# One layer of a hybrid decoder on one core: the column spans of its dense products

## The reference, cut to what matters

```python
xn = rmsnorm(x, attn_norm_g)
gq, gk, gv, gg, glr, dq, dk, dv = split(xn @ w_in)          # 1024 x 3088
log_a = log_sigmoid(glr @ w_gk2 + b_gk) / 16                # rank 16
gla_o = gated_linear_attention(gq, gk, gv, log_a)           # 4 heads
diff_o = differential_attention(rope(rmsnorm(dq)), rope(rmsnorm(dk)), dv)   # 4 heads, paged cache for the samples
h = x + concat(rmsnorm(gla_o) * silu(gg), rmsnorm(diff_o) * 0.8) @ w_out    # 1024 x 1024
hn = rmsnorm(h, ffn_norm_g)
h = h + (silu(hn @ w_ffn_gate) * (hn @ w_ffn_up)) @ w_ffn_down              # 1024 x 2816, twice, and back
gate = sigmoid(rmsnorm(h, ple_norm_g) @ w_ple_gate)         # 1024 x 1024
h = h + gate * (p @ w_ple_proj)                             # 256 x 1024
```

## Time and profile before

| | |
|---|---|
| median of 3 runs | 2168.06 us (2166.67 to 2168.38) |
| span of the profiled execution | 2161.1 us |
| median less span | 7.0 us |
| TensorE matmuls | busy 1927.8 us, 13348 instructions |
| VectorE, ScalarE, GpSimd | busy 972.4, 605.6, 404.4 us |
| mean granted TensorE clock | 0.943 |

### The profile page before, as it was taken

One profiled execution on the slowest core, in us unless ns is written; L12 is line 12 of the kernel. 1 busy time (PEld: TensorE's weight loads), 2 busy tenths in 40 slices (PEclk: granted clock), 3 DMA queues, 4 the chain that ended last, 5 costly groups with the idle time before them and its releaser, 6 DMA issues. The chain is left out here.

```text
span 2161.1 us, 36230 instructions
## 1 busy us (share of the span) xinstructions
PE 1927.8 (89%) x13348; PEld 1743.4 (81%) x13348; DVE 972.4 (45%) x1364; ACT 605.6 (28%) x1011; POOL 404.4 (19%) x398
## 2 busy tenths in 40 slices
PE   5999998556887789888789899999999999999798
PEld 4999998543555566656589899999999999999798
DVE  4224611784666545555533523433343334335543
ACT  4113312531444444444432211111111111112420
POOL 1112321331000234343311100110111011102210
PEclk9999999785878999999999999999999999999899
DMA  4323521005300799999721111111111111110221
GB/s 130 102 80 101 154 70 50 21 3 192 113 1 0 247 378 387 387 387 387 250 61 40 49 49 39 49 40 50 39 48 42 49 40 39 50 50 20 66 75 42
DMA packets 187844, 236.56 MB, mean 109 GB/s; under 512 B 12994, under 2 KB 127635, under 8 KB 187731
## 3 DMA queue, kind: packets, MB, share of 16 engines
q1 hardware_dynamic: 167250, 167.81, 24.3%
q0 software_dynamic: 20480, 67.13, 8.4%
HBM read 213.49 MB, written 16.92 MB: 107 GB/s over the span
## 5 line engine op out<-in xcount | busy, mean ns | idle before, releaser
L150 PE MATMUL psum<-h_hi,w_hi 128*128 128x364 f32 x1248 | 279.2, 332 | 2.5 <-issue 2.5
L150 PE MATMUL psum<-h_lo,w_hi 128*128 128x364 f32 x1248 | 276.6, 330 | 0.0
L150 PE MATMUL psum<-h_hi,w_lo 128*128 128x364 f32 x1248 | 275.4, 329 | 0.0
L2051 ACT ACTIVATE w_hi<-w_raw 128x1024 fp32r<-128x1024 f32 x66 | 68.9, 1060 | 584.4 <-PE psum L150 566.1
L150 PEld LDWEIGHTS psum<-h_hi,w_hi 128*128 128x128 f32 x1248 | 215.6, 189 | 4.6 <-issue 4.4
L150 PEld LDWEIGHTS psum<-h_lo,w_hi 128*128 128x128 f32 x1248 | 217.5, 189 | 0.0
L150 PEld LDWEIGHTS psum<-h_hi,w_lo 128*128 128x128 f32 x1248 | 217.1, 189 | 0.0
L2027 POOL TENSOR_TENSOR w_raw<-w_raw,gains 128x1024 f32<-128x1024 f32 x42 | 80.3, 1913 | 652.2 <-DMA w_raw<-in_w_ffn_gate 352.2
L150 PE MATMUL psum<-x_hi,w_hi 128*128 128x364 f32 x792 | 187.6, 345 | 11.1 <-DVE x_lo L1884 7.3
L1081 POOL DMA_DIRECT2D dec_v<-in_cache_v x256 | 138.0, 539 | 266.4 <-issue 263.3
L150 PE MATMUL psum<-x_hi,w_lo 128*128 128x364 f32 x792 | 176.4, 331 | 0.0
(11 more groups left out here) (268 smaller groups left out, 2831.3 us busy)
## 6 DMA issues: line engine op xcount, KB each, us to landing
dec_v<-in_cache_v POOLq DMA_DIRECT2D x256, 256.0 KB, 5.7
dec_k<-in_cache_k SPq DMA_DIRECT2D x256, 256.0 KB, 8.8
w_raw<-in_w_in SPq DMA_DIRECT2D x25, 512.0 KB, 3.9
w_raw<-in_w_ffn_gate SPq DMA_DIRECT2D x22, 512.0 KB, 3.9
w_raw<-in_w_ffn_up SPq DMA_DIRECT2D x22, 512.0 KB, 3.8
w_raw<-in_w_ffn_down SPq DMA_DIRECT2D x22, 512.0 KB, 4.1
feat_swap<-feat_n SPq DMA_DIRECT2D x32, 136.5 KB, 2.4
x_in<-in_x_prompt SPq DMA_DIRECT2D x4, 1024.0 KB, 8.1
```

The source lines that it names most:

```text
L150: ins = pe.matmul(out[:, c, 0:SPAN], w(k), x(k)[:, c * SPAN:c * SPAN + SPAN], start=n == 0 and w is whi and x is xhi, stop=n == len(ks) - ...
L2051: act.activation(m.whi[:, slot], m.raw[:, u], ACT.Copy).then_inc(s["w_hi"], 1)
```

## The change

The 1092 columns of a dense product are cut at 512 and 1024: the spans have 512, 512 and 68 columns. The first two fill their banks wholly, so the three banks hold 1092 adjacent elements, and every evacuation reads them as one run. Number, operands and order of the matmuls are the same. L454 and the row sums (L1711) keep pieces of 364.

```diff
-def spans(ap):
-
-    return ap.rearrange("p (c n) -> p c n", n=SPAN)
+CUTS = [(0, 512), (512, 512), (1024, T - 1024)]
+
+
+def whole(bank):
+
+    return bank.rearrange("p c n -> p (c n)")[:, 0:T]
...
-            for c in range(3):
-                ins = pe.matmul(out[:, c, 0:SPAN], w(k), x(k)[:, c * SPAN:c * SPAN + SPAN],
+            for c, (at, width) in enumerate(CUTS):
+                ins = pe.matmul(out[:, c, 0:width], w(k), x(k)[:, at:at + width],
                                 start=n == 0 and w is whi and x is xhi, stop=n == len(ks) - 1 and w is wlo)
...
-                    act.activation(spans(m.f[:, u]), dense[u][:, :, 0:SPAN], ACT.Copy).then_inc(evacuated, 1)
+                    act.activation(m.f[:, u], whole(dense[u]), ACT.Copy).then_inc(evacuated, 1)
...
-                for c in range(3):
-                    ins = pe.matmul(dense[pr][:, c, 0:SPAN], m.gk2[:, pr * P:pr * P + P],
-                                    m.g[0:16, low, c * SPAN:c * SPAN + SPAN], start=True, stop=True)
+                for c, (at, width) in enumerate(CUTS):
+                    ins = pe.matmul(dense[pr][:, c, 0:width], m.gk2[:, pr * P:pr * P + P],
+                                    m.g[0:16, low, at:at + width], start=True, stop=True)
...
-                dve.tensor_tensor(spans(m.h[:, n]), spans(m.h[:, n]), dense[n % 2][:, :, 0:SPAN], ALU.add
+                dve.tensor_tensor(m.h[:, n], m.h[:, n], whole(dense[n % 2]), ALU.add
                                   ).then_inc(s["evacuated"], 1)
```

More of the change, by code:

```diff
@@ L391, in _ @@
                 else:
-                    act.activation(spans(m.g[:, 0, :]), dense[0][:, :, 0:SPAN], ACT.Copy).then_inc(evacuated, 1)
+                    act.activation(m.g[:, 0, :], whole(dense[0]), ACT.Copy).then_inc(evacuated, 1)
                 hi(s + 2, u)
@@ L397, in _ @@
                     act.wait_ge(product_done, s + 1)
-                    act.activation(m.g[:, bass.ds(2 * i + (1 + v), 1), :].rearrange("p o (c n) -> p (o c) n", n=SPAN),
-                                   dense[1 - v][:, :, 0:SPAN], ACT.Copy).then_inc(evacuated, 1)
+                    act.activation(m.g[:, bass.ds(2 * i + (1 + v), 1), :].rearrange("p o t -> p (o t)"),
+                                   whole(dense[1 - v]), ACT.Copy).then_inc(evacuated, 1)
                     hi(s + 2, 1 - v)
@@ L403, in _ @@
                 act.wait_ge(product_done, s + 1)
-                act.activation(spans(m.g[:, s - 16, :]), dense[s % 2][:, :, 0:SPAN], ACT.Copy).then_inc(evacuated, 1)
+                act.activation(m.g[:, s - 16, :], whole(dense[s % 2]), ACT.Copy).then_inc(evacuated, 1)
         @block.tensor
@@ L696, in _ @@
                 act.wait_ge(s["z_done"], pr + 1)
-                act.activation(spans(m.t1[:, pr]), dense[pr][:, :, 0:SPAN], ACT.Abs, bias=gain(m, "bgk")[:, pr:pr + 1]
+                act.activation(m.t1[:, pr], whole(dense[pr]), ACT.Abs, bias=gain(m, "bgk")[:, pr:pr + 1]
                                ).then_inc(s["sp_abs"], 1)
@@ L880, in _ @@
                 dve.wait_ge(s["sp_abs"], pr + 1)
-                dve.tensor_scalar(spans(m.t2[:, pr]), dense[pr][:, :, 0:SPAN], gain(m, "bgk")[:, pr:pr + 1], 0.0,
+                dve.tensor_scalar(m.t2[:, pr], whole(dense[pr]), gain(m, "bgk")[:, pr:pr + 1], 0.0,
                                   ALU.add, ALU.min).then_inc(s["sp_min"], 1)
@@ L2145, in scaled @@
                 dve.wait_ge(s["product_done"], x + 1)
-                dve.tensor_tensor(spans(dst), dense[bank][:, :, 0:SPAN], spans(m.rb[:, :]), ALU.mult
+                dve.tensor_tensor(dst, whole(dense[bank]), m.rb[:, :], ALU.mult
                                   ).then_inc(s["evacuated"], 1)
@@ L2401, in scaled @@
                 dve.wait_ge(s["gate_done"], n + 1)
-                dve.tensor_tensor(spans(m.gt), dense[0][:, :, 0:SPAN], spans(m.rb[:, :]), ALU.mult
+                dve.tensor_tensor(m.gt, whole(dense[0]), m.rb[:, :], ALU.mult
                                   ).then_inc(s["gate_scaled"], 1)
@@ L2409, in result @@
                     dve.wait_ge(s["filled"], n * 3 + (PT - 3))
-                dve.tensor_tensor(spans(m.gp[:, u]), spans(m.gt), dense[1][:, :, 0:SPAN], ALU.mult
+                dve.tensor_tensor(m.gp[:, u], m.gt, whole(dense[1]), ALU.mult
                                   ).then_inc(s["gated"], 1)
```

## The result

The changed kernel takes 2356.7 us (median of 4 runs, 2353.57 to 2362.37), the kernel before 2168.16 (4 runs, 2166.67 to 2168.38): a ratio of 1.0881, with a 95% interval of 1.0864 to 1.0898. It is slower by 188.5 us; 186 were forecast, and 2354 us.

The account below looks back on a forecast made before the run. TensorE's dense matmuls (L150) were taken as the bound: 2616 groups of three at +73 ns give +191 us, less 5 us hidden in waits, so 2168 + 186 = 2354 us; range 2295 to 2419 us.

Parts of the forecast that it names:

- TensorE's pace in L150 is the whole of it: Dense products: 2616 groups of three matmuls take 1305 us of the span, and TensorE waits for nothing in it.
- The load needs 107 to 112 ns and lies under the short matmul alone: Dense products: the next weight load fits only under the 68 columns, so that matmul takes 112 ns, not 28.3.
- The wide slots: Each 512-column matmul of the dense products was taken as 230 ns, between a floor of 213 and 234.
- the two readings: The extra beyond streaming columns: fixed at 14.6 ns gives 228 ns for 512 columns, growing with columns gives 234.
- The sum: Three matmuls sharing weights: 572 ns against 499, +191 us over 2616 groups, less 5 us filling TensorE's waits at stage starts.
- The 7.0 us around the program: Median 2168.06 us lies 7.0 us over the span of 2161.1; this was taken as around the program and staying.
- The evacuations are free: PSUM evacuations: one run of 1092 elements in place of three of 364 gives nothing, taken as 0.
- What would show it: FFN profile signs: groups 0.57 us apart, about 0.11 after the 68-column start, 7848 loads, tile of 72 matmuls 13.7 us.
- The hidden load: Rival, dense products: TensorE holds more than one load ahead, so no change, 2168 us; chance 0.08.
- The half load: Rival, dense products: a float32r load needs one cycle a column, short slot 58 ns, about 2215 us; chance 0.06.
- plain float32: Rival, dense products: narrow float32r runs in two passes with a load each, short slot 224 ns, 2647 us; chance 0.03.
- The clock: Rival, dense stages: granted clock falls to half for a tenth of the time, some +125 us on top; chance 0.01.

Follow-up runs that it names:

- The four widths: Last matmul of 68, 132, 196 or 240 columns in place of the kernel before's 364, evacuation in one run: 2356.7, 2283.8, 2215.0 and 2165.8 us.
- 288: Spans of 288, 512 and 292 columns, evacuated in one run, against the kernel before with three of 364: 2166.4 us, ratio 0.9999.
- 292: Spans of 292, 512 and 288 columns, evacuated in one run, against the kernel before with three of 364: 2165.2 us, ratio 0.9998.

## Why the prediction was right

*TensorE's pace in L150 is the whole of it.* Right: 207 us more of TensorE's busy time (by records that overlap), 194 us more of span, no new wait of weight between the engines.

*The load needs 107 to 112 ns and lies under the short matmul alone.* Right, and the term that carries the forecast. L781 was the row to read: it has the slot (112 ns) though it computes in plain float32. The four widths give 110 to 112, the two loads in a row 108. That the slot is the load's, and no other distance between matmuls, is supported by the loads' starts but was not tested by itself.

*The wide slots.* 230 was taken, 232 measured, 2 x 2 ns under. A column costs 0.4446 ns and a matmul 4.6 on top, so of the two readings (a fixed extra of 14.6, an extra that grows) it was nearly the growing one, 234.

*The sum.* 572 ns forecast, 575 from the starts; +76 ns a triple, times 2616 +199 us, of which the kernel shows 194 in the span. So 5 us were taken back, as forecast, and all of it on balance in the last stage: `embedding` with the turn to it grew by 13 us, where 240 triples at 76 ns are 18. The span thus grew by 194 us for 186, 3 ns a triple more than forecast.

*The 7.0 us around the program.* Wrong, and this is where the close hit, 2354 against 2356.7, has luck in it. In every run whose span is on record the time is 1.6 to 1.7 us over the span (2356.68 and 2355.0 for the profile after). So the profiled execution of the kernel before took some 2163 us, 5 under the median of 2168, and most of the 7.0 us is the distance between two executions. Of the 8 us by which the sum fell short in the span, these 5 don't show in the medians, and 3 are left. Which part of an execution varies was not tested; the time at half clock does vary, from 247 to 298 us between the profiles of kernels equally fast to 0.4%, and most of it lies in gla and the attentions.

*The evacuations are free.* Right: with 288 and 292 no short matmul is left and the evacuations are still joined, and the ratios are 0.9999 and 0.9998, within 0.1%.

*What would show it.* Wrong in one point. The prediction wanted about 0.11 us after a 68-column start, and named a start within 60 ns of it as a sign that the load is hidden. The start comes after 31 ns, and the load is not hidden. By the loads' starts, the record of this matmul begins before its weights are in place; the wait shows in the step after it, 312 in place of 232 ns, and in the loads' own starts. By its own words the prediction would have been refuted by a row that in truth confirms it. The sum of the three steps, which it also named (0.57 us), is what holds. The other signs (7848 records, evacuations of 1.08 and 1.29 us, the clock row but for two 8s) came as written; a tile of 72 came out at 13.8 us (24 x 575 ns) for 13.7.

*The rivals.* The hidden load asked for two loads in hand: the load row at 1500.42 starts only when the one at 1500.32 is done, and a short matmul in the middle of the wide ones costs as much. The half load (2215 us) needed a slot of 58, plain float32 (2647 us) more than 7848 records. The clock was 1.00 in the 600 us of FFN, and over the span 0.942 for 0.943.

## What to carry to other kernels

Where every matmul brings its own 128-column float32r weights, let no matmul move fewer than about 240 columns: at full clock the shorter ones (68, 132 and 196 measured) took some 111 ns, the time of the next load, whatever their own columns needed. So cut columns evenly, or at least above that width, and don't fill PSUM banks for the sake of one long evacuation, which gained nothing here. Before you take the distance between a profile's span and a median for a fixed cost, compare it with the same distance in other runs. When a trace has no row for a form, look for the row that shares the resource: a plain float32 matmul of 64 columns with full weights gave this price to within 2 ns.

## What the runs showed of the hardware

Between 364 and 512 columns a float32r column costs 0.4446 ns at full clock, 7% over the 0.417 of 2.4 GHz; at half clock it costs the full cycle and no more (427 ns for 512). Spans that start 8 bytes past a multiple of 16 in the activations cost 0.4 to 0.6% of the kernel, 4 to 6 ns a triple in FFN. A load of the weights that TensorE already has costs as much as one of new weights (2359.2 us against 2356.7). And the start of a record is not always the start of streaming: behind the 68 columns the next matmul is recorded about 80 ns early, if the load's length is what holds it.
